# Delta rule stage: level transposes by VectorE instead of TensorE, and two weight splits a head by GpSimd

## The reference, cut to what matters

```python
def gated_delta_rule_chunked(q, k, v, beta, g):
    ...
    kb = k * beta[..., None]
    Lmat = jnp.where(strict, jnp.einsum('bhnid,bhnjd->bhnij', kb, k) * decay, 0.0)
    eye = jnp.eye(C, dtype=Lmat.dtype)
    rhs = jnp.concatenate([v * beta[..., None], kb * jnp.exp(gc)[..., None]], axis=-1)
    sol = lax.linalg.triangular_solve(eye + Lmat, rhs, left_side=True, lower=True, unit_diagonal=True)
    ...
def deltanet_mixer(h, w_in, conv_w, A_log, dt_bias, onorm_g, w_out):
    p = h @ w_in
    ...
    qkv = jax.nn.silu(causal_dwconv(qkv, conv_w))
```

## Time and profile before

| | us |
|---|---|
| median of 3 runs | 1892.54 (1891.99 to 1892.97) |
| the profiled execution | 1893.59 |
| its span | 1891.8 |
| TensorE busy | 1868.5 (99% of the span), granted clock 0.999 |
| VectorE busy | 1217.1 (64%) |
| ScalarE busy | 791.2 (42%) |
| GpSimd busy | 304.7 (16%) |
| the delta stage's heads | from about 660 to 960 |

### The profile page before, as it was taken

One profiled execution on the slowest core, in us unless ns is written; L12 is line 12 of the kernel. 1 busy time (PEld: TensorE's weight loads), 2 busy tenths in 40 slices (PEclk: granted clock), 3 DMA queues, 4 the chain that ended last, 5 costly groups with the idle time before them and its releaser, 6 DMA issues.

```text
span 1891.8 us, 29791 instructions
## 1 busy us (share of the span) xinstructions
PE 1868.5 (99%) x10616; PEld 1524.4 (81%) x10616; DVE 1217.1 (64%) x1898; ACT 791.2 (42%) x1491; POOL 304.7 (16%) x225
## 2 busy tenths in 40 slices
PE   9999999999999999999999999999999999999998
PEld 7888888888888767777778888888877888888886
DVE  6997564333334877777746847747779568376474
ACT  5234453232233655555534424424547444243242
POOL 0532232111012300001011101101222211011012
PEclk9999999999999999999999999999999999999999
DMA  5223313232323112111112332322421223322232
GB/s 210 89 101 101 134 58 121 89 101 89 106 94 97 49 61 70 62 52 62 51 61 97 103 108 78 106 94 89 134 68 46 72 85 111 101 91 98 89 102 76
DMA packets 48547, 170.49 MB, mean 90 GB/s; under 512 B 5408, under 2 KB 7616, under 8 KB 48320
## 3 DMA queue, kind: packets, MB, share of 16 engines
q1 hardware_dynamic: 47248, 165.12, 26.2%
q10 hardware_dynamic: 1200, 3.95, 0.6%
HBM read 166.94 MB, written 2.11 MB: 89 GB/s over the span
## 4 chain that ended last, share of the span: by engine, by line
PE 90%; DVE 6%; ACT 2%; issue 1%; POOL 0%; DMA 0%; DVEq 0%; SPq 0%; ACTq 0%; POOLq 0%
PE ps L280 19%; PE ps L282 18%; PE ps L281 18%; PE ps L268 9%; PE ps L270 9%; PE ps L269 9%; PE ps L800 1%; PE ps L825 1%; PE ps L732 1%; DVE scr L1659 1%; PE ps L319 1%; DVE scr L1650 1%; DVE Y L1650 1%; ACT Y L1582 0%; PE ps L870 0%
## 5 line engine op out<-in xcount | busy, mean ns | idle before, releaser
L227 ACT ACTIVATE w_hi<-w_raw 128x1024 fp32r<-128x1024 f32 x302 | 315.1, 1052 | 261.4 <-PE ps L282 171.9
L232 DVE TENSOR_TENSOR w_lo<-w_raw,w_hi 128x1024 fp32r<-128x1024 f32 x253 | 344.1, 1363 | 122.9 <-ACT w_hi L227 122.2
L280 PE MATMUL ps<-A_hi,w_hi 128*128 128x512 f32 x882 | 359.7, 408 | 2.2 <-DVE Y L1140 1.1
L282 PE MATMUL ps<-A_hi,w_lo 128*128 128x512 f32 x882 | 344.6, 391 | 0.0
L281 PE MATMUL ps<-A_lo,w_hi 128*128 128x512 f32 x882 | 343.8, 390 | 0.0
L280 PE MATMUL ps<-B_hi,w_hi 128*128 128x512 f32 x680 | 267.8, 394 | 1.3 <-DVE B_lo L1177 0.9
L282 PE MATMUL ps<-B_hi,w_lo 128*128 128x512 f32 x680 | 264.8, 389 | 0.0
L281 PE MATMUL ps<-B_lo,w_hi 128*128 128x512 f32 x680 | 264.6, 389 | 0.0
L280 PEld LDWEIGHTS ps<-A_hi,w_hi 128*128 128x128 f32 x882 | 165.6, 188 | 38.4 <-DVE Y L1140 2.5
L282 PEld LDWEIGHTS ps<-A_hi,w_lo 128*128 128x128 f32 x882 | 165.5, 188 | 35.4
L268 PE MATMUL ps<-A_hi,w_hi 128*128 128x512 f32 x488 | 190.2, 390 | 0.0
(11 more groups left out here) (318 smaller groups left out, 2610.7 us busy)
## 6 DMA issues: line engine op xcount, KB each, us to landing
w_raw<-d_ws SPq DMA_DIRECT2D x304, 512.0 KB, 3.5
X<-d_xT SPq DMA_DIRECT2D x4, 512.0 KB, 8.3
X<-d_xT ACTq DMA_DIRECT2D x1, 2048.0 KB, 8.2
d_out<-X SPq DMA_DIRECT2D x8, 256.0 KB, 2.3
scr<-gc_rows ACTq DMA_DIRECT2D x7, 256.0 KB, 3.1
cst<-d_cst SPq DMA_DIRECT2D x1, 800.0 KB, 11.7
par<-d_par SPq DMA_DIRECT2D x1, 344.5 KB, 2.9
scr<-d_pw SPq DMA_DIRECT2D x1, 256.0 KB, 11.7
```

What stands on the lines that cost most here:

```text
L227: nc.scalar.activation(w_hi[:, c], raw[:, c], ACT.Copy).then_inc(S(f"w_hi{s}"), 1)
L232: nc.vector.tensor_tensor(w_lo[:, c], raw[:, c], w_hi[:, c].bitcast(F32), ALU.subtract)\
L280: pe.matmul(ps[bank][:], w_hi[:, c], hi, start=k == 0, stop=False)
L282: last = pe.matmul(ps[bank][:], w_lo[:, c], hi, start=False, stop=k == total - 1)
```

## The change

In levels 2 to 5 the products with the identity (L809) and their copies by ScalarE (L972) are gone. In their place VectorE transposes the factor `TC` into `TTC` after the subtraction of levels 1 to 4: one transpose of 128 partitions for the first pair, two of 64 partitions for the second, whose halves are kept crosswise. They are transposes within blocks of 32x32; up to level 5 nothing of the factor lies outside of these. They signal `d_tr64`, for which L825 of the next level waits. The low parts of slots 2 and 3 leave VectorE (four operations of 512 columns a head) and are done by GpSimd (two of 1024 columns), after its first power. Level 6 is as it was. `LEAD` is 2.

```diff
@@ crossed_level, TensorE
-                if l > 1:
-                    for n in range(2):
-                        for b in range(2):
-                            for i in range(2):
-                                last = pe.matmul(square64(ps[6 + i], n, b ^ i), square64(TC, 2 * i + n, b),
-                                                 ident64[64 * b:64 * b + 64, :], start=True, stop=True)
-                                if n and b:
-                                    last.then_inc(S("d_ttr"), 1)
                 fill(l, 0)
                 for i in range(2):
                     pe.wait_ge(S("d_x"), at("d_x", 2 * l + 3 + i))
                     if l > 1:
-                        pe.wait_ge(S("d_ttc"), at("d_ttc", 2 * (l - 2) + i + 1))
+                        pe.wait_ge(S("d_tr64"), at("d_tr64", 3 * (l - 1)))
@@ delta_act, ScalarE
-                    n = 2 * (l - 1) + i + 1
-                    act.wait_ge(S("d_ttr"), at("d_ttr", n))
-                    if l < 5:
-                        a.activation(pair64(TTC, i), ps[6 + i][:, 0:P], ACT.Copy).then_inc(S("d_ttc"), 1)
-                    else:
+                    if l == 5:
+                        act.wait_ge(S("d_ttr"), at("d_ttr", i + 1))
@@ delta_dve, VectorE
-                if l == 1:
-                    split(0, 0)
-                elif l == 2:
+                if l == 2:
                     conv(0, 0)
...
-                if l == 1:
-                    split(0, 1)
-                elif l == 2:
-                    split(1, 0)
-                elif l == 3:
-                    split(1, 1)
+                if l < 5:
+                    dve.wait_ge(S("d_pt"), at("d_pt", 2 * l))
+                    dve.wait_ge(S("d_tt"), at("d_tt", 2 * l + 2))
+                    v.transpose(pair64(TTC, 0), pair64(TC, 0)).then_inc(S("d_tr64"), 1)
+                    for b in range(2):
+                        v.transpose(pair64(TTC, 1)[half_of(1 - b)], pair64(TC, 1)[half_of(b)])\
+                            .then_inc(S("d_tr64"), 1)
+                if l == 3:
                     dve.wait_ge(S("d_sq"), at("d_sq", 2 * NCH))
@@ delta_pool, GpSimd
             nc.gpsimd.tensor_tensor(TK[:, 24:28], TK[:, 4:8], mhalf[:, 4:8], ALU.pow).then_inc(S("d_sqk"), 1)
+            for k in range(LEAD):
+                split_lo_pool(pool, rnd(U_DELTA, h + 1) + (k + LEAD) // SLOTS, (k + LEAD) % SLOTS)
             pool.wait_ge(S("d_oms"), at("d_oms", 1))
```

More of the change, by code:

```diff
@@ L657, in build @@
                    d_gram=2, d_s1=4, d_sq_eps=1, d_sqk=1, d_mask=1, d_dt=4, d_eg=1, d_la=5, d_kvr=12, d_tt=14, d_t=3,
-                   d_px=12, d_x=16, d_pt=12, d_ttr=10, d_ttc=12, d_pw=2, d_wt=2, d_pv=4, d_vn=4,
+                   d_px=12, d_x=16, d_pt=12, d_ttr=2, d_ttc=4, d_tr64=12, d_pw=2, d_wt=2, d_pv=4, d_vn=4,
                    d_po=1, d_ps=3, d_s=3, d_osq=4, d_oms=1, d_orow=1, d_o1=4, d_ro=1, d_o2=1, o_hi=1, o_lo=1)
@@ L845, in delta_pe @@
                     pe.wait_ge(S("d_x"), at("d_x", 2 * l + 3 + i))
-                    pe.wait_ge(S("d_ttc"), at("d_ttc", 8 + 2 * (i + 1)))
+                    pe.wait_ge(S("d_ttc"), at("d_ttc", 2 * (i + 1)))
                     for c in (2 * i, 2 * i + 1):
@@ L1110, in delta_dve @@
                     conv(0, 3)
-                else:
+                elif l == 6:
                     conv(1, 0)
```

## The result

| | before | after |
|---|---|---|
| median of 6 runs each, taken side by side | 1892.4 us | 1931.06 us (1928.99 to 1932.25) |
| ratio, 95% interval | | 1.0201 (1.0191 to 1.0211) |
| span of the profiled execution | 1891.8 us | 1928.4 us |
| granted TensorE clock, mean over the span | 0.999 | 0.986 |

The change costs 38.7 us. The forecast was 1908.0 with a range of 1895 to 1914: the sign was right, and more than half of the cost was missing from it. After the change L825 is L817, L1090 is L1079, L1092 is L1081, L1097 is L1086, L1118 is L1105, L1036 is L1025, and the new transposes are L1112 and L1114.

A forecast was written before the change was run, and what follows sets the result against it. TensorE, busy 99% of the span, was taken as the bound. Removed products (-7.0), mask (+3.4) and GpSimd holding VectorE (2 x 2.18 + 5 x 2.10 + 4.2) gave +15.5 us: 1908.0 us, range 1895 to 1914.

The forecast's parts named there:

- the sum: Over the delta stage's eight heads: -7.0 + 3.4 + 2 x 2.18 + 5 x 2.10 + 4.2 = +15.5 us.
- My rivals: VectorE's hold by GpSimd: costs nothing (1889 us, chance 0.13), partly held (1896, 0.08), held twice in every head (1923, 0.07).
- Products removed, -7.0: L809 gone from levels two to five of eight heads: 0.22 us each off TensorE's path, 7.0 us.
- Transposes at nothing: VectorE's added transposes after levels one to three, 0.95 us each level, cost TensorE nothing, with 0.12 us to spare.
- The 128x4 operation: VectorE's 0.16 us operation after level three uses up the spare time; its cost was taken as zero.
- The mask, 0.49 a head: Decay mask behind level four's transposes makes TensorE wait 0.49 us in seven heads: 3.4 us; bounds 0 and 4.3.
- The port: Ahead of level one GpSimd holds VectorE; TensorE waits 2.10 us in heads 2-6, 2.18 in 0-1, 4.2 in 7.
- The extension from 512 to 1024 columns: A 1024-column GpSimd operation keeps VectorE out for its whole length, though the widest seen held had 512.
- GpSimd's second operation: From 747.2 to 749.6 us, beside VectorE operations with PSUM input or one-input transposes only: free.

The follow-up runs named there:

- filled kernel: Changed kernel, collision kept, plus 12 unused products of 128x384 (24 in head 7) where TensorE waits ahead of level one: 1912.92 us, ratio 1.0107.
- late kernel: Changed kernel with one more GpSimd wait, so its low parts start behind both crossing masks of level one: 1893.36 us, ratio 1.0004.
- halves of 512: Changed kernel with each GpSimd low part split into two operations of 512 columns: 1908.75 us, ratio 1.0078.
- low parts alone: Kernel before with only the two low parts moved to GpSimd, products and ScalarE copies kept: 1929.13 us, ratio 1.0189.
- transposes alone: Changed kernel with the two low parts back on VectorE between the levels: 1908.66 us, ratio 1.0081.
- mask moved: GpSimd's low parts started behind level one's masks, decay mask moved ahead of level four's subtraction, later convolution steps moved on: 1890.84 us, ratio 0.9989.
- new wait order: Changed kernel, GpSimd's low parts behind level one's masks; TensorE waits once and first for transposes, then for crossing masks: 1889.94 us, ratio 0.9986.
- the last: Changed kernel, GpSimd's low parts late, transposes waited for once and first, decay mask moved, 128x4 operation moved to level one: 1887.20 us, ratio 0.9972.

## Why the prediction was wrong

**The step that failed is the sum.** It priced TensorE's idle at its own length: 2.10 us of waiting, 2.10 us of time. The granted clock was in no term of it, though its mean stood in the profile. The kernel before had 0.999, since nothing in the stage let TensorE stand for long (1.05 us at most); the change put idles of 2 us and more in a stream without any, and that is a condition under which the rows of before said nothing on the clock. The filled kernel shows at least 18.1 us for it, more than the 17.1 by which the range was missed: without the clock it would have been 1912.9 at most, inside the range. My rivals all varied the length of the wait, none what a wait brings with it.

**Products removed, -7.0:** held in size. The pitch is 2.54 where nothing is late. But see the next.

**Transposes at nothing: mis-sized.** The prediction found 0.12 us to spare and took zero, and named the bound itself. Three small errors go the same way. From the start of the subtraction to that of the next mask it is 748.58 - 747.18 = 1.40 in the late kernel, 0.04 more than the 1.36 that I had. From mask to products it is 0.74 with the new waits and not the 0.58 of the earlier trace rows, which was read at level one, where they are absent. The 128x4 operation was left out knowingly. In the late kernel's head 2 this makes 0.10 + 0.09 + 0.15 over levels two to four, about 0.34 a head, or 2.7 us.

**The mask, 0.49 a head: mis-sized.** 0.61 was measured in seven heads; the bound of the prediction was 0.61. With the last rows it is 3.23 - 2.54 = 0.69 in the late kernel. Together the two terms come to 1.0 a head, which takes back the 0.88 a head that the products give: the late kernel, at 1.0004, has the time of the kernel before.

**The port: held, point by point.** L1081 at 2.85 us (2.86 worked out), idles of 2.02 (2.10) in the middle heads and 4.11 (4.2) in head 7, with both operations held there and for the reason given. Heads 0 and 1 show 2.53 and 2.54, of which 0.37 stood there before: 2.17, against 2.18. The extension from 512 to 1024 columns was right, and the halves of 512 confirm it from the other side. GpSimd's second operation was free, as said.

**The account.** 1892.8, less 7.0 for the products, plus 7.5 for transposes and mask (1893.36 - 1892.82 + 7.0, by the late kernel), plus 2 x 2.17 + 5 x 2.02 + 4.1 = 18.5 for the port: 1911.8. The filled kernel's 1912.92 less its own 0.7 is 1912.2. From there to 1931.06 it is 18.8 to 19.3 us for the clock.

**What stays open.** Why the clock stays low for 3.4 us behind one idle and for over 6 behind another of the same length, and why it once did not fall at all, no run here tells. Nor is it settled why a deficit of 25.6 us costs only 18 to 19.3. A part of the deficit lies in the idle itself (in head 7 some 1.4 us), and a TensorE at half clock comes later to levels where it else had waited a little for VectorE; the shares were not measured.

## What to carry to other kernels

Idle time on TensorE has two prices: its length, and the granted clock behind it. Where a change puts idles of the size seen here (1.5 to 4 us) in a stream that had none, work out the sum once more with a stretch at half clock behind each, and look at the granted clock by stages before anything else in the profile after. Before work goes to GpSimd, list the VectorE operations with two SBUF inputs that lie beside it and whose turn is just then: the same two operations cost 38 us over the kernel in one place, and next to nothing where they start behind the last such operation of that stretch and end before the next. And where an engine waits for several things, try it with one wait for what has long been done, put first: that gave 3.4 us here.

## What the runs showed of the hardware

- **The clock follows idle, and not in proportion.** Idles of 0.95 us five times left the granted clock at 1.00; two of 1.46 us and all eight of 2.02 us and more in the kernel after brought it to 0.50; one of 2.03 us in the kernel with low parts alone did not. While it is at 0.50 the three products of a dense block start 0.43 us apart (756.79 to 757.22) in place of 0.23 (750.58 to 750.81). 20.9 us of idle in 33 pieces of up to 1.0 us lowered it once, 19.3 us in eight pieces seven times. Nor does it take a long idle: at the end of head 7, behind waits of 0.32 and 0.55 us, the clock fell in four kernels (at 993.9 with the low parts alone, 971.7 with the transposes alone, 971.0 with halves, 954.6 with the mask moved), and stayed at 1.00 behind the same waits in the kernel before, in the late one, in the one with the new wait order and in the last.
- **Products of no use can be worth their place.** 108 of them, 20.1 us of TensorE, in time that was idle anyway: 18.1 us gained.
- **One GpSimd operation holds a VectorE operation with two SBUF inputs for its whole length**, at both lengths that were run: 0.69 becomes 2.85 us beside 1024 columns and 1.78 beside 512. Operations with a PSUM input and transposes ran beside GpSimd at their usual length: L1086 at 0.48 or 0.49, L1112 at 0.31, L1114 at 0.64 or 0.65.
- **How TensorE's waits are arranged costs time**: a wait for the transposes behind each mask's wait gives 2.64 us from level to level, one wait ahead of both gives 2.54. Whether order or number does it is not shown.
